# When a weight buffer is given back: a wait on the products' own counters, or a mark that TensorE sets after its own wait

## The reference, cut to what matters

```python
def ada_modulation(cond, w, b):
    mod = jax.nn.silu(cond) @ w + b                  # (1024) @ (1024, 6144), per layer
...
for layer in range(DEPTH):                           # 2
    ... six modulation rows for context and for latent tokens
    if layer % N_MIXERS == 0:                        # layer 0: multi-head latent attention
        q, ckv, kr = mla_compress(h, w_in, q_norm, w_uq, kv_norm)   # h @ w_in, then @ w_uq
        out = mla_attend(q, ckv, kr, w_ukv, w_o)     # ckv @ w_ukv, softmax, @ w_o
    else:                                            # layer 1: neighbourhood attention
        q, k, v = nat_qkv(h, w_qkv)
        out = ... @ w_o
    x = x + gate * out
    x = x + gate * grouped_moe(...)                  # router, gate/up, down
```

## Time and the profile before

| | |
|---|---|
| median of three executions | 1335.31 us |
| the profiled execution | 1334.99 us, span 1333.1 us |
| mean granted TensorE clock | 0.987 of full speed |
| TensorE busy | 1252.3 us, 94% of the span |
| VectorE, ScalarE, GpSimd busy | 591.3, 331.4, 229.4 us (44%, 25%, 17%) |
| DMA | 266.83 MB, mean 200 GB/s |

### The profile page before, as it was taken

How to read it: one execution, slowest core, us unless ns; L and a number is a source line. 1 busy time by engine, 2 the same in 40 slices (tenths; PEclk the granted TensorE clock), 3 DMA queues, 4 the chain that set the end, 5 groups by cost and what they waited for, 6 DMA issues and landing times.

```text
span 1333.1 us, 20023 instructions
## 1 busy us (share of the span) xinstructions
PE 1252.3 (94%) x7823; PEld 721.9 (54%) x7823; DVE 591.3 (44%) x1510; ACT 331.4 (25%) x783; POOL 229.4 (17%) x296
## 2 busy tenths in 40 slices
PE   4999999999999999998889999999999999999995
PEld 3665466666645654444444455565885455444442
DVE  5222256556625664444352000001884666444445
ACT  4121344444402400000022000001982340000002
POOL 6220500010010011122220100004221001221230
PEclk9999999999999999999999999999999999999998
DMA  9412311231475469999772273136226336999966
GB/s 377 187 41 96 157 65 65 73 121 65 191 261 188 159 238 386 383 378 393 207 229 103 102 263 127 64 127 205 78 70 221 164 127 238 382 385 376 347 157 212
DMA packets 45165, 266.83 MB, mean 200 GB/s; under 512 B 6948, under 2 KB 13428, under 8 KB 31232
## 3 DMA queue, kind: packets, MB, share of 16 engines
q1 hardware_dynamic: 22672, 192.85, 36.9%
q0 software_dynamic: 16640, 51.73, 14.0%
q10 hardware_dynamic: 5760, 20.97, 4.1%
HBM read 230.19 MB, written 33.76 MB: 198 GB/s over the span
## 4 chain that ended last, share of the span: by engine, by line
PE 77%; DMA 12%; DVE 6%; issue 2%; ACT 2%; ACTq 0%; DVEq 0%; SPq 0%; POOLq 0%
PE PS L911 13%; DMA xrows<-big,info 11%; PE PS L1280 10%; PE PS L1127 10%; PE PS L1173 10%; PE PS L1190 6%; PE PS L1030 5%; PE PS L778 4%; PE PS L784 3%; PE PS L800 3%; PE PS L1070 3%; PE PS L1339 2%; PE PS L992 2%; PE PS L1302 1%; DVE big L1687 1%
## 5 line engine op out<-in xcount | busy, mean ns | idle before, releaser
L1127 PE MATMUL PS<-weights,ht 128*128 128x512 f32 x320 | 142.4, 596 | 0.9 <-DVE ht L1687 0.9
L1280 PE MATMUL PS<-ht,weights 128*128 128x128 f32 (+1 forms) x512 | 139.8, 434 | 0.0
L911 PE MATMUL PS<-weights,ht 128*128 128x336 f32 (+1 forms) x320 | 117.6, 526 | 1.6 <-ACT ht L1464 1.6
L1173 PE MATMUL PS<-big 128*128 128x512 f32 x256 | 115.0, 601 | 4.1 <-DVE big L2140 4.1
L778 PE MATMUL PS<-const,big 128*128 128x128 f32 (+2 forms) x611 | 89.8, 282 | 25.1 <-DVE big L2149 4.7
L778 PEld LDWEIGHTS PS<-const,big 128*128 128x128 f32 (+2 forms) x611 | 72.4, 142 | 72.8 <-issue 37.8
L1280 PEld LDWEIGHTS PS<-ht,weights 128*128 128x128 f32 x512 | 77.7, 191 | 62.1 <-issue 62.1
L1594 ACT ACTIVATE big<-PS 128x256 f32<-128x256 f32 x34 | 13.0, 384 | 335.3 <-PE PS L1173 335.3
L1127 PEld LDWEIGHTS PS<-weights,ht 128*128 128x128 f32 x320 | 59.0, 190 | 68.2 <-issue 68.2
L911 PEld LDWEIGHTS PS<-weights,ht 128*128 128x128 f32 x320 | 61.2, 194 | 53.0 <-issue 39.4
L1687 DVE TENSOR_TENSOR big<-PS,big 128x512 f32<-128x512 f32 (+1 forms) x70 | 44.2, 672 | 98.3 <-PE PS L1190 49.8
(11 more groups left out here) (255 smaller groups left out, 1798.3 us busy)
## 6 DMA issues: line engine op xcount, KB each, us to landing
weights<-in_ada SPq DMA_DIRECT2D x22, 2048.0 KB, 7.9
big<-in_gu SPq DMA_DIRECT2D x16, 2048.0 KB, 19.1
weights<-in_gu SPq DMA_DIRECT2D x12, 2048.0 KB, 21.8
rows<-in_down SPq DMA_DIRECT2D x18, 1024.0 KB, 11.8
weights<-in_down SPq DMA_DIRECT2D x16, 1024.0 KB, 16.6
ht<-in_gu SPq DMA_DIRECT2D x6, 2048.0 KB, 21.5
weights<-in_qkv SPq DMA_DIRECT2D x6, 2048.0 KB, 11.0
weights<-in_wo SPq DMA_DIRECT2D x4, 2048.0 KB, 8.4
```

The lines of the kernel that those rows point to most:

```text
L911: ins = pe.matmul(bank(4 + u % 2, n), lhs(k), rhs(k), start=(k == 0), stop=(k == ks - 1))
L1127: ins = pe.matmul(bank(4 + j), OT[:, k, t * P:(t + 1) * P], w[j][:, k, :], start=(k == 0), stop=(k == KD - 1))
L1173: ins = pe.matmul(bank(0), gatT[:, k, :], w[:, k, :], start=(k == 0), stop=(k == KD - 1))
L1280: ins = pe.matmul(bank(bb, n1 - n0), w[:, k, m * P:(m + 1) * P], hT[:, k, n0:n1], start=(k == 0), stop=(k == KD - 1))
```

## The change

SP no longer looks at the products' counters. Three new semaphores, `w_used[0..2]`, one for each slot that is filled more than once, count how often the slot has been used up. After the last product of each weight PE waits for that product itself (a wait on the counter that its own last matmul raises) and then executes a `nop` that counts up `w_used`. For slots 3 and 4 there is no `nop`, but in `ada` the wait stands there all the same. Where two pieces share a loop (`win`, `wo`), both are released together behind the last unit. `products_done` and `last_in` are gone.

```diff
+        w_used = [sem(f"w_used{i}") for i in range(3)] + [None] * 2
...
-        def products_done(what, l, j):
...
             def static_load(g, n):
+                if w_rank(g, n):
+                    sp.wait_ge(w_used[SLOTS_[g][n]], w_rank(g, n))
...
-                if w_rank(g, n):
-                    sp.wait_ge(*products_done(*last_in(slot, g, n)))
...
                 def static_done(slot):
-                    return products_done(*last_in(slot, l, len(LOADS[l])))
+                    return sum(x.count(slot) for x in SLOTS_[:l + 1])
...
-                sp.wait_ge(*static_done(2))
+                sp.wait_ge(w_used[2], static_done(2))
...
         def _(pe):
+            def release(what, l=0, j=0):
+                if w_used[w_slot(what, l, j)[0]] is not None:
+                    pe.nop().then_inc(w_used[w_slot(what, l, j)[0]], 1)
...
             def ada(l, j):
                 ins.then_inc(m_mm, 1)
+                pe.wait_ge(m_mm, i + 1)
+                release("ada", l, j)
...
                  if u in (4, 5, 7, 9):
                     lat_transposes((4, 5, 7, 9).index(u))
+            pe.wait_ge(g_mm, AT_MM["win"] + 2 * NT)
+            release("win", 0, 0)
+            release("win", 0, 1)
...
                              for kt in range(6):
                                 ins = transpose(PS[0:ROPE, kt * P:(kt + 1) * P], krw[:, kt, :])
                             ins.then_inc(l_tr, 1)
+                pe.wait_ge(g_mm, AT_MM["uq"] + (j + 1) * 10)
+                release("uq", 0, j)
...
             def k_heads(p, b0=4):
                 ins.then_inc(k_mm, 1)
+                if p == H // 2 - 1:
+                    pe.wait_ge(k_mm, p + 1)
+                    release("ukv")
...
                      if l == 0 and t < 4:
                         ada(1, t)
+                pe.wait_ge(g_mm, AT_MM[name] + 2 * NT)
+                release(name, 0, 0)
+                release(name, 0, 1)
...
                  if u in (5, 7, 9):
                     ada(1, 5 + (5, 7, 9).index(u))
+                if u >= 8:
+                    pe.wait_ge(g_mm, AT_MM["vproj"] + u + 1)
+                    release("qkv", 0, u - 4)
...
                  ins.then_inc(qk_mm, 1)
+                if n % 4 == 3:
+                    pe.wait_ge(qk_mm, n + 1)
+                    release("qkv", 0, u // 4)
                 if n in ADA_QK:
                     ada(1, 8 + ADA_QK.index(n))
```

More of the change, by code:

```diff
@@ L510, in _ @@
                     load_dn(1)
-                sp.wait_ge(*static_done(0))
+                sp.wait_ge(w_used[0], static_done(0))
                 load_gu(2)
@@ L516, in _ @@
                 if l == 0:
-                    sp.wait_ge(*static_done(1))
+                    sp.wait_ge(w_used[1], static_done(1))
                     load_gu(3)
```

## The result

| | before | after |
|---|---|---|
| median (nine executions each) | 1335.88 us | 1343.22 us |
| lowest to highest | 1334.99 to 1337.28 | 1337.64 to 1346.36 |
| ratio | | 1.0051, 95% interval 1.0036 to 1.0067 |
| profiled execution (span) | 1334.99 (1333.1) | 1338.73 (1336.9) |

The change makes the kernel 7.3 us slower. The forecast was 1343.3. The profiled execution of the changed kernel lies 4.5 us under its median, so the two spans differ by 3.8 us only, and the profile is read place by place.

A forecast was written before the change was run, and what follows sets the result against it. PE's matmuls were taken to bound the kernel, so waits there are mostly paid in full: 1.9 + 0.84 + 1.5 + 2.35 + 1.0 + 0.1 + 0.31 = 8.0 us, on 1335.31 giving 1343.3 us; range 1339.8 to 1347.5.

The forecast's parts named there:

- Kind A: Place behind an `ada` or `k_heads` with one condition after the wait: 0.07 + 0.06 + 0.08 = 0.21 us.
- Kind G: Place inside a stream of units, more conditions after the wait: 0.16 + 0.06 + 0.08 + 0.10 + 0.10 = 0.50 us.
- A2: Place behind an `ada` or `k_heads` with more conditions after the wait: 0.31 us.
- the 0.1 of `win`: Behind the last `win` unit: wait met during five transposes, leaving two nops and weights not loaded ahead, 0.1 us.
- The `wo` places: Two places costed at nothing, covered by a 0.73 us wait for DVE's normed rows; 0.6 us each without it.
- The loads: SP's second `uq` load goes out later, 12 us to spare; the third `qkv` load keeps its 1.8 us.
- The front, 0.31: One `ada` of the front, number 1, goes straight on with transposes on the chain: 0.31 us.
- Hidden: Rival: waits hidden because PE has work queued or stages end on another engine; 1335.3 to 1338 us, chance 0.04.
- half hidden: Rival: layer 0's attention and the front absorb their waits; 5.8 us, 1341.1 us, chance 0.08.
- the fall of the clock: Rival: one drop of the granted clock as in 645 to 698 us, 3.2 us more, 1346.5 us, chance 0.03.
- A late load: Rival: a load tight by 1.8 us slips in traffic, stalling 2 to 5 us; 1346 to 1348 us, chance 0.05.
- Faster, by shorter scatters: Rival: shifted weight loads shorten eleven scatters in layer 0's experts, 11 us back, 1332.3 us, chance 0.02.

The follow-up runs named there:

- nops alone: Changed kernel without TensorE's waits for its own product, 37 nops kept, SyncE on the products' counters as before: 1335.38 us beside 1334.15 for the kernel before, ratio 1.0000.
- more waits: Kernel before, plus a TensorE wait for its own product behind each of the 52 units of `gemm_unit`, no nop: 1349.67 us beside 1334.46, ratio 1.0114.
- waits alone: Changed kernel without the nops, TensorE's waits kept at 36 places, SyncE on the products' counters as before: 1339.09 us beside 1334.15 for the kernel before, ratio 1.0025.
- the experiment with the load alone: Kernel before, but SyncE starts the second `uq` load after the transposes behind the last `win` unit, some 5 us later: 1334.08 us beside 1334.46, ratio 1.0003.

## Why the prediction was right

**Forecast 1343.3, range 1339.8 to 1347.5, measured 1343.22.** The measured difference of the two medians is 7.3 us (4.8 to 9.0 by the interval), the sum was 8.0, and the stretches of the profile give 8.2. That the forecast lies within 0.1 us is luck: the median before is 0.57 higher with nine executions than with three, and the difference 0.7 lower than the sum. What the runs bear out is the mechanism and the price of each place.

- *The wait for its own product is the price.* Shown: nops alone nothing (ratio 1.0000), waits moved behind the next work nothing (0.9998), more waits more (1.0114). More exactly it is the work missing behind the product while PE waits, as the waits behind the next work show (U 19.26 against 20.03).
- *Kind A, 0.21.* Measured 0.22 in H. Its parts were not quite those of the sum: 0.15 for the wait where 0.13 was taken, 0.07 for the nop where 0.08 was.
- *Kind G, 0.50.* Measured 0.55. 0.33 for the wait (0.32 taken), 0.07 for the nop, and 0.15 for the further conditions where 0.10 was taken, with 0.14 as the upper bound. This was the mis-sized term, as was A2 with it (0.31 taken, 0.37 measured). The estimate of 0.10 was the difference of two hand-offs; what counts is the number of semaphore instructions from the wait on, at 0.15 each after the first.
- *The stages.* `uq` and attention 2.9 forecast, 3.25 measured (the 0.1 of `win` lies ahead of this stretch); output projection 0.84 and 0.88; values 1.5 and 1.59; queries and keys 2.35 and 2.50. Two places were put into the wrong kind. The first `ada` of the attention is A2 and not A: the gap behind it is 0.33 us (156.55), as against 0.18 behind the other seven. And only one of the four `ada` of the queries and keys is A2, not two: one gap of 0.33 and three of 0.18. The two errors cancel in the sum.
- *The `wo` places cost nothing, for the reason named.* The zeroing starts 0.33 us late after a gap (454.95), the wait for DVE's rows behind it shrinks from 0.73 to 0.19 (461.11), and what is left of the stretch is the four `ada`, 0.88. The cover was nearly used up.
- *The loads.* The second `uq` was issued 4 us and more later and hidden, as worked out; the experiment with the load alone shows it.
- *The front, 0.31, and `win`, 0.1.* Neither shown nor refuted: the front differs from one execution to another by more than that.
- *The rivals.* Hidden and half hidden are refuted by H. So is the fall of the clock: the granted clock of the three windows of the earlier trace rows is 1.00, 0.97 and 1.00 after the change (1.00, 0.94 and 1.00 before), and the run with 52 waits has 1.00 where 41 of them stand. A late load is seen nowhere. Faster, by shorter scatters, isn't seen: the experts of layer 0 with what surrounds them are 0.22 us shorter in one profile.
- *What the profile would show.* The gap behind the `ada` was forecast to 0.14 behind the modelled end and is 0.18; the matmul after it is shorter in turn, and the sum of both is right. The first matmul of a G place was to take 0.10 us more and takes 0.07 (667 ns, 595 before; 697 with the waits alone). The queries and keys were to be 2.3 us longer and are 2.5.

What stays open: why the granted clock of the first 46 us differs between executions. The 1.40 us by which the rest behind 932.45 is shorter are no work of the change: this rest takes 405.85 us in the profile before, 406.7 with the nops alone and 403.9 with the later load, where the code of this part is that of the kernel before but for the nops.

## What to carry to other kernels

Don't let the engine that sets the pace wait for its own last result just to tell another engine that a buffer is free: let the other engine wait on the counter that the last instruction raises anyway. If a mark of its own is needed, put wait and mark behind the next piece of work, so that this work stands ahead of the wait; here 1.7 us of it (four records of 0.43) were enough. And where an engine must stop, count the semaphore instructions that stand between the stop and its next work. Here each behind the first cost 0.15 us, half of the stop itself inside a stream (0.33) and as much as the stop behind an `ada` (0.15).

## What the runs showed of the hardware

- A `nop` that counts up a semaphore and the wait ahead of it are one instruction in TensorE's part of the trace (51 ns, at 846.76 us behind `ada(1, 9)` of the changed kernel). 37 nops without a wait cost nothing (ratio 1.0000, 0.9983 to 1.0017; H 26.61 against 26.62, U 19.27 against 19.26). Behind a wait for the own product with no matmul in between the first cost 0.07 us and each further one about 0.15.
- TensorE's waits alone cost 0.15 us behind an `ada` and 0.33 inside a stream of units (from U; 0.32 in the stream of `uq` with a wait behind each unit). Behind an `ada` the next matmul takes 697 ns in the kernel before already; inside the stream it takes 595 ns before and 697 with the waits alone.
- A wait for the own product that holds cost nothing where two matmuls stood between the product and the wait: the instruction with the wait came 0.04 to 0.07 us after the product's modelled end, as in the changed kernel, and U, which has two such places, was 19.26 as before.
